# State-space outputs by feature, with decays read back by DMA and two weight triangles as separate products

## What is computed

```python
SSD_HEAD_DIM, SSD_HEADS, SSD_GROUPS, SSD_STATE, SSD_CHUNK = 64, 32, 8, 128, 128

def ssd_chunked(x, dt, a, bm, cm, h0, need_y):
    xc = x * dt[..., None]                              # by chunk of 128 tokens
    cs = jnp.cumsum(dt * a, axis=chunk_tokens)
    ...
    seg = cs[:, :, :, None] - cs[:, :, None, :]
    lmat = jnp.exp(jnp.where(lower, seg, -jnp.inf))
    cb = jnp.einsum('bclgn,bcsgn->bclsg', cc, bc)
    y = (jnp.einsum('bclsg,bclsgr,bcsgrp->bclgrp', cb, lmat, xc)
         + jnp.einsum('bclgn,bcgrpn,bclgr->bclgrp', cc, h_in, jnp.exp(cs)))

def ssd_output(yf, yb, xs, z, ssd_d, ssd_norm_g, w_ssd_o):
    y = (yf + yb + ssd_d[:, None] * xs).reshape(b, n, SSD_D_INNER)
    return rmsnorm(y * jax.nn.silu(z), ssd_norm_g) @ w_ssd_o
```

## Time and profile before

| | |
|---|---|
| median of 3 runs | 2561.36 us (2559.42 to 2563.14) |
| the profiled execution | 2561.69 us, span 2559.9 us |
| TensorE (PE) busy | 2478.0 us, 97% |
| weight loads (PEld) | 2146.7 us, 84% |
| GpSimd (POOL) busy | 1495.2 us, 58% |
| VectorE (DVE) busy | 1224.3 us, 48% |
| ScalarE (ACT) busy | 1125.1 us, 44% |
| DMA | 314.03 MB, 123 GB/s in the mean |
| granted TensorE clock | 0.992 of full |

### The profile page before, as it was taken

How to read it: one execution, slowest core, us unless ns; L and a number is a source line. 1 busy time by engine, 2 the same in 40 slices (tenths; PEclk the granted TensorE clock), 3 DMA queues, 4 the chain that set the end, 5 groups by cost and what they waited for, 6 DMA issues and landing times.

```text
span 2559.9 us, 38883 instructions
## 1 busy us (share of the span) xinstructions
PE 2478.0 (97%) x15118; PEld 2146.7 (84%) x15118; DVE 1224.3 (48%) x2582; ACT 1125.1 (44%) x2371; POOL 1495.2 (58%) x1318
## 2 busy tenths in 40 slices
PE   8999999999899999999999999999989999989998
PEld 7779998885688888888888888888958888889997
DVE  3545502236747888874233112121365788843311
ACT  2345533115526777674022002042364766654543
POOL 1019775870354554543985888865314666668786
PEclk9999999999999999999999999999999999999999
DMA  7566453237532222214322333333463233265554
GB/s 211 181 188 187 133 156 112 83 95 259 194 99 67 75 58 66 75 50 156 95 87 83 99 99 99 99 99 99 133 201 99 83 99 91 69 150 171 168 200 140
DMA packets 365718, 314.03 MB, mean 123 GB/s; under 512 B 13648, under 2 KB 342386, under 8 KB 364530
## 3 DMA queue, kind: packets, MB, share of 16 engines
q1 hardware_dynamic: 361586, 298.80, 39.2%
q10 hardware_dynamic: 3392, 12.59, 1.3%
q0 software_dynamic: 576, 0.43, 0.2%
HBM read 304.45 MB, written 7.34 MB: 122 GB/s over the span
## 4 chain that ended last, share of the span: by engine, by line
PE 81%; DVE 7%; issue 4%; POOL 3%; DMA 2%; ACT 2%; POOLq 0%; SPq 0%; DVEq 0%; ACTq 0%
PE PS L729 39%; PE PS L1131 10%; PE PS L787 5%; PE PS L1138 4%; PE PS L1361 3%; POOL rounded L2767 3%; PE PS L752 3%; DVE mid_a L2489 2%; PE PS L1172 2%; PE PS L1259 2%; PE PS L680 2%; PE PS L1181 2%; PE PS L1059 1%; PE PS L951 1%; PE PS L1047 1%
## 5 line engine op out<-in xcount | busy, mean ns | idle before, releaser
L2767 POOL TENSOR_TENSOR rounded<-ring,rounded 128x512 fp32r<-128x512 f32 (+1 forms) x872 | 1114.3, 1310 | 726.3 <-ACT rounded L1413 415.6
L729 PE MATMUL PS<-rounded 128*128 128x256 f32 (+1 forms) x6096 | 1044.8, 334 | 10.6 <-POOL rounded L2767 7.3
L729 PEld LDWEIGHTS PS<-rounded 128*128 128x128 f32 x6096 | 926.9, 191 | 123.2 <-POOL rounded L2767 6.5
L2790 POOL TENSOR_TENSOR rounded<-ring,constants 128x512 fp32r<-128x512 f32 x216 | 229.3, 1092 | 247.1 <-PE PS L729 124.1
L1131 PE MATMUL PS<-rounded 128*128 128x512 f32 (+1 forms) x1536 | 343.4, 380 | 5.7 <-DVE mid_a L2489 5.1
L1131 PEld LDWEIGHTS PS<-rounded 128*128 128x128 f32 x1536 | 275.4, 188 | 60.8 <-DVE mid_a L2489 3.7
L1413 ACT ACTIVATE rounded<-ring 128x2048 fp32r<-128x2048 f32 (+1 forms) x99 | 180.0, 1822 | 128.9 <-DMA ring<-in_w_mlp_dram 45.7
L2489 DVE SCALAR_TENSOR_TENSOR mid_a<-PS,V,mid_a 128x510 f32<-128x510 f32 (+3 forms) x256 | 182.2, 714 | 25.5 <-ACT mid_a L1742 18.0
L1780 ACT ACTIVATE rounded<-constants,big 128x128 fp32r<-128x128 f32 x384 | 150.2, 391 | 0.0
L1780 ACT ACTIVATE rounded<-constants,mid_v 128x128 fp32r<-128x128 f32 x384 | 150.2, 391 | 0.0
L1138 PE MATMUL PS<-rounded 128*128 128x256 f32 x1152 | 147.7, 286 | 0.0
(11 more groups left out here) (277 smaller groups left out, 3209.8 us busy)
## 6 DMA issues: line engine op xcount, KB each, us to landing
ring<-in_w_mlp_dram SPq DMA_DIRECT2D x64, 1024.0 KB, 5.5
ring<-in_w_in_dram SPq DMA_DIRECT2D x56, 1024.0 KB, 5.4
ring<-in_ada_w_dram SPq DMA_DIRECT2D x48, 1024.0 KB, 5.3
ring<-in_w_in_dram SPq DMA_DIRECT2D x81, 512.0 KB, 4.1
ring<-in_w_up_dram SPq DMA_DIRECT2D x44, 512.0 KB, 5.2
ring<-in_w_ssd_o_dram SPq DMA_DIRECT2D x16, 1024.0 KB, 6.0
ring<-in_w_out_dram SPq DMA_DIRECT2D x12, 1024.0 KB, 5.2
ring<-in_w_down_dram SPq DMA_DIRECT2D x16, 704.0 KB, 4.9
```

What stands on the lines that cost most here:

```text
L729: mm = pe.matmul(PS[:, b, 0:cols], w[:, k, m * P:(m + 1) * P], x(half * kt + k), start=(half == 0 and k == 0 and n_pass == 0), stop=(half ...
L2767: ins = pool.tensor_tensor(lo[:, r], raw[:, r], hi[:, r], ALU.subtract)
L2790: ins = pool.tensor_tensor(hi[:, r], raw[:, r], ones[:, 0:1].broadcast_to([P, 512]), ALU.mult)
```

## The change

The outputs of a chunk are computed with features on partitions. Per head both triangles get a product of their own, and so does each direction's starting state, all added up in one place: the stationary operand is x by token or the starting state, 64 columns wide, the moving one the 128x128 weights. Two heads share a 128-partition result, one in the lower, one in the upper 64 partitions.

The decays come another way. `decay_sums` makes the running sums by head as rows too; they are stored to memory once a layer, and `fetch` reads a group's rows of one chunk back, the same to all 128 partitions. ScalarE makes the exponentials from them: relu(start - row) keeps the argument in bounds (CAP), dt enters as a logarithm. VectorE multiplies by the masked scores, GpSimd multiplies C by the decays of the starting states (`scaled_c`). z is produced by feature; the norm's sums of squares over features are added up by GpSimd (`add_squares`) and summed by one product with ones; its inverse is applied to the gates after the projection rather than before it.

```diff
@@ decays read by DMA
+        decay_sums_of = [nc.dram_tensor(f"decay_sums{l}", (TT, 2 * SSD_HEADS, P), F32, kind="Internal").ap() for l in range(LAYERS)]
+        def decays_of(l, g, t):
+            of_heads = decay_sums_of[l][t].rearrange("(d h) n -> d (h n)", d=2)[:, g * GH * P:(g + 1) * GH * P]
+            return of_heads.unsqueeze(0).broadcast_to([P, 2, GH * P])
@@ TensorE: decay_sums
+                    for d, sums in enumerate((t_le, t_ge)):
+                        r = slice(32 * d, 32 * d + 32)
+                        mm = pe.matmul(PS[r, 4 + t, 256:256 + P], dta[:, t, r], sums, start=True, stop=True)
@@ TensorE: product, z
-                            t0 = (2 * (n - 4) + t) * P
+                            m = (n - 4 + e) * P
-                                    mm = pe.matmul(PS[:, b, t * GW:(t + 1) * GW], x[:, k, t0:t0 + P], w[:, k, :],
+                                    mm = pe.matmul(PS[:, b, e * q_cols:(e + 1) * q_cols], w[:, k, m:m + P], x[:, k, 0:q_cols],
@@ TensorE: seg
-                    for lhs, parts in zip(tri, seg_parts):
-                        for part in parts:
-                            mm = pe.matmul(PS[:, 7 - t % 2, :], lhs, part, start=part is seg_parts[0][0],
-                                           stop=part is seg_parts[1][1])
@@ TensorE: chunk
+                    for j in range(2):
+                        terms = [(xtok[:, t, :], ex[t % 2][:, d, :]) for d in range(2)]
+                        terms += [(hin[:, h, :], decay_rows[rows_of_chunk[t]][:, d, :]) for d, h in starts_of(t)]
+                        for n, (lhs, rhs) in enumerate(terms):
+                            for e in range(2):
+                                r = 2 * j + e
+                                mm = pe.matmul(PS[e * HD:(e + 1) * HD, 7 - j, cols], lhs[:, r * HD:(r + 1) * HD],
+                                               rhs[:, r * P:(r + 1) * P], start=(n == 0), stop=(n == len(terms) - 1))
@@ TensorE: after the last turn
-                pe.wait_ge(*c.need(tok_scaled, ny))
-                for f in range(YT):
-                    turn_scaled(f)
+                pe.matmul(PS[:, 4, 0:q_cols], ones, ctanh_b[:, 0:q_cols], start=True, stop=True).then_inc(*c.made(y_summed))
@@ ScalarE: decays
-                    act.activation(PS[:, 7 - t % 2, :], PS[:, 7 - t % 2, :], ACT.Exp).then_inc(*c.made(e_ready))
-                                act.activation(seg_parts[d][n][:, r * P:(r + 1) * P], mask, ACT.Copy,
-                                               scale=dta_parts[n][:, t, h:h + 1]).then_inc(*c.made(seg_in))
+                    act.wait_ge(*c.sofar(decays_loaded[rows_of_chunk[t]]))
+                    for d in range(2):
+                        for r in range(GH):
+                            h, m = 32 * d + g * GH + r, slice(r * P, (r + 1) * P)
+                            ins = act.activation(ex[t % 2][:, d, m], rows[:, d, m], ACT.Relu, scale=-1.0, bias=start_of[:, t, h:h + 1])
+                    act.activation(ex[t % 2], ex[t % 2], ACT.Exp, scale=-1.0, bias=cap[:, 0:1]).then_inc(*c.made(e_ready))
+                    act.activation(part, part, ACT.Exp).then_inc(*c.made(c_decays))
@@ VectorE: weights and outputs
-                        step(dve.scalar_tensor_tensor(out=m, in0=cb_lo[:, t, :], scalar=dt[:, t, g * GH + r:g * GH + r + 1], in1=m,
-                    dve.tensor_tensor(ex[:, t % 2, :], dt_up[:, t % 2, :], PS[:, 7 - t % 2, :], ALU.mult).then_inc(*c.made(m_ready))
+                    for d, cb in enumerate((cb_lo, cb_up)):
+                        e = per_head(ex[t % 2][:, d, :])
+                        dve.tensor_tensor(e, e, bc_mid(cb[:, t, :], GH), ALU.mult).then_inc(*c.made(g_ready))
+                        dve.scalar_tensor_tensor(out=yg[l][:, f, :], in0=chans[l][p][:, 1 - j, 0:q_cols], scalar=skip_d[:, l, f:f + 1],
+                                                 in1=PS[:, 6 + j, 0:q_cols], op0=ALU.mult, op1=ALU.add).then_inc(*c.made(y_read))
@@ GpSimd: scaled_c
+                            e = per_head(decay_rows[rows_of_chunk[t]][:, d, :])
+                            ins = pool.tensor_tensor(e, e, bc_mid(chans[l][p][:, 3, t * P:(t + 1) * P], GH), ALU.mult)
@@ ScalarE, after the last turn: rounded parts straight from yg, no transposes
+                        act.activation(y_hi[l][:, f, :], yg[l][:, f, :], ACT.Copy, scale=col("ssd_norm_g_2", l * YT + f))\
+                            .then_inc(*c.made(hi_ready))
```

488 lines of the change are left out of this document (241 added, 247 removed).

## The result

| | median, us | runs | ratio to before, 95% interval |
|---|---|---|---|
| before | 2562.1 | 4 | 1 |
| changed | 2534.7 (2533.2 to 2536.8) | 4 | 0.9897 (0.9885 to 0.9910) |

The change makes the kernel 27 us, 1.0%, faster. Forecast were 57.6 us and 2504 us, with a range of 2490 to 2530: the direction was right, half of the gain did not come, and the time lies outside the range. The profiled execution of the changed kernel took 2533.2 us with a span of 2531.4, 28.5 less than before; its stretches are compared here.

What follows compares the result with a forecast made beforehand. TensorE, 81% of the chain, was taken as the bound. Layer 0 turns 27.5, layer 1 turns 9, waits 8, tails 12 and 6.5, less added 3.4 and 2, gave 57.6 us off 2561.7: 2504 us, range 2490 to 2530.

Steps and rivals of the forecast that it cites:

- every cover grows: In the group loops other engines get more slack; VectorE's late convolutions in layer 1 come on time, 8 us gained.
- the turn of layer 0: Sign for layer 0's group loop: a turn of 45.0 us without idle; forecast wrong if not between 44 and 46.
- Side by side: Chunk products: two 64-column halves overlap fully, 0.055 us a record; chunks of 2.06 or 1.62 us, 92 us in all.
- rivals A and B: Chunk halves do not overlap, 2581 us, chance 0.09; or overlap only partly, 2524 us, chance 0.12.
- Rival B: Chunk halves overlap only partly, a step of 0.14 us, streaming 97 us instead of 77; 2524 us, chance 0.12.
- z by feature: Layer 0's z in 48 products of 512 columns: 1.1 us a group, 9 us gained; layer 1 nothing.
- Layer 1's turns: Layer 1's group loop: 1.1 us a group, 9 us, plus 8 us from vanishing waits; turn near 34 us.
- Tail of layer 0: Before layer 0's output projection, token norms and 128 turned products go; 3 us waiting for gate 7's eviction; 12 us gained.
- Tail of layer 1: Before layer 1's output projection, 64 turned products and a wait go; 0 if slabs decide, 6.5 us gain taken.
- Added work: Two 32-column products a chunk for stored sums, 0.42 us each time, 3.4 us; operations before each layer's fence, 2 us.
- rival C: Reading one memory row by 128 partitions is slow, ScalarE waits for decay rows in layer 0; 2544 us, chance 0.07.
- Rival D: Both tails give nothing because ScalarE's and VectorE's copies and rests stand in the open; 2523 us, chance 0.07.

Runs made afterwards that it cites:

- e1: Changed kernel with GpSimd's scaled_c(2) moved ahead of the rests of the next group's slabs in a turn; 2512.6 us, ratio 0.9816.
- e5: Kernel of e4 with all of a chunk's products for the first 64-column half before those for the second, not alternating; 2518.1 us, ratio 0.9828.
- e4: Changed kernel with the moves of e1, e2 and e3 together; 2503.0 us, ratio 0.9766.
- e7: Changed kernel with GpSimd's products of C with decay rows cut to 8 of 128 columns, only time read; 2508.9 us in one run.
- e2: Changed kernel with gate tile 7's eviction in layer 0's tail moved ahead of ScalarE's wait for rests and rounding; 2529.6 us, ratio 0.9867.
- e3: Changed kernel, layer 1's tail: transfers back issued behind the last gained rows, slab 2 rounded after eight rests; 2527.3 us, ratio 0.9866.

## Why the prediction was wrong

**The step that failed** is "GpSimd swaps products of the same size and adds two sums of squares a group. So every cover grows". It looked at what each engine has to do in a turn and not at the order in which GpSimd does it, nor at the new number of products. With an order in which two slab rests stand ahead of a product that TensorE needs first, the cover was gone in six of eight turns: 14.3 us of waiting, of the 17 us that layer 0's loop missed by. e1 gave it back (14.8). The text had named the turn of layer 0 as the test, 44 to 46 us; it was 48.3, and is 45.35 once the order is mended.

**Side by side (rivals A and B).** Refuted as costs of the chunk: 1.90 and 1.46 us are below the 2.06 and 1.62 summed. For two halves in this kernel the records show no loss: a pair of records starts about every 0.11 us (eight records, 992.71 to 993.14), and one record alone takes no less in e5 (four, 994.24 to 994.73). But the forecast's evidence was misread. The 3.6 times for L680 set a row's length (12 records of 256 columns in 2.75 us) against starts; by starts those 12 take 2.40 us, 1042.26 to 1044.66, so 0.20 each and 3.2 us for 16, which against L680's 1.01 is 3.2 times for four. Rival B drew on the Trainium skill, page "TensorE: Matmul & The Clock Gate", section "Measured speedup vs the span model", with 2.38 times for three column tiles, which is 79% of ideal. The trace agrees with that share for four, 3.2 of 4 being 80%, where the prediction said that it did not.

**z by feature** was mis-sized. 3.22 + 3.22 us were the lengths of rows, tails included, though the text itself warns of them. By starts the term is 0.7 us a turn and not 1.1. All pieces of a turn by starts, before and in e4: the sums give 4.2 us, the chunks cost 1.1 (5.6 before, 6.7 after), z gives 0.6, and the four other input products cost 0.6 more (22.1 before, 22.7 after), three of them next to split products. That makes 3.1 (48.4 to 45.35) where 3.4 were summed; over the loop 25.1 (e1) of 27.5. So what the chunks are cheaper than forecast is paid by their neighbours.

**Layer 1's turns** gave 13.6 of 17 us. The turn is near the forecast 34 (34.3), but the waits for VectorE did not go (3.4 us of 5.1 left), because VectorE does not get the relief that was summed: its weights were bounded by 0.62 and 1.08 us and take 1.36 in layer 0 and 1.18 in layer 1, above the upper bound, with GpSimd busy beside it; and the last step of silu, which the change does not touch, went from 1.10 to 1.39 us on `ctanh_b` and from 1.12 to 1.31 on `constants` in layer 1. e7 shows the coupling. In the last turn new waits of 2.4 and 2.0 us stand where those of 1.7 and 1.0 were.

**Tail of layer 0.** Forecast 12, measured 10.8. The mechanism was the one named, gate 7's eviction behind the rests; the wait was 5.5 and not 3, and 4.15 us of it were program order (e2).

**Tail of layer 1.** Forecast 6.5, measured 1.5. The lower bound, 0 "if slabs decide", was the right case. The step missed that the transfers back stand behind VectorE's last rest and meet the slabs there; with them issued early the tail gives 7.4 (e3, 50.2 to 42.8). Which of the three makes the slabs late was not tested; the windows above speak for the 4 KB of the last gate.

**Added work.** The 32-column sums cost 0.46 us each where 0.42 were summed (from the sums to the next projection product 1.50 us after, L1107 to L739, against 1.04 before, L1097 to L729). The fence cost nothing in place of 2: from the last sums to the loop it takes 3.7 us with 0.34 of new products in it, against 3.5 before, and in layer 1 it is shorter.

**The fetch (rival C)** cost nothing, as forecast: ScalarE has no wait for it, and the median landing time is 4.9 us for 512 KB, against 4.1 in the earlier trace rows. **Rival D**, tails without gain, came true in one tail of two.

**The clock** was in no term. TensorE was granted half clock for 42.7 us of the profiled execution before and for 61.7 after, 19.0 more, which is at most 9.5 us of lost work. Of these 19.0 us 5.1 lie in the 8 tiles, 10.2 between them and layer 1's loop, and 4.7 in the end; the tails have 2.4 more and the first row 3.4 less. In the last two the clock fits the growth of 3.5 and 2.7 us: e4, with 10.2 and 5.2 us at half clock there against 13.7 and 5.1 before, takes 627.1 and 242.6 us, as before. In the 8 tiles it does not, for they stay at 134.3 us with the clock full (e2, e4); there the late rests cost as much. The mean granted clock was 0.992 in the profiled execution before; of the four runs after none was above 0.988, and in e4, without the new waits, all five stood at 0.991. In e1, without those of layer 0's loop, it went from 0.986 to 0.990, so the waits are not the whole of it.

With the three orders mended (e4) the kernel takes 2503.0 us; the forecast of 2504 was for a kernel without them. That it lies so close is partly luck: the sum had 3 to 4 us too much for z and the same for layer 1's waits and nothing for the late rests in the 8 tiles (2.4), and too little for the tails (14.9 us in layer 0 and 8.5 in layer 1 in e4) and the fence.

## What to carry to other kernels

Where work moves to an engine that had slack, follow that engine's program order through one turn and ask when each result is due; a sum of its busy time does not show a product that stands behind work for the next turn. Ask the same of transfers: when they can be issued, and what else wants the DMA engines then. A wait that names the engine that prepares a weight slab may only pass on a late landing, so test it by moving the transfer and the preparation apart. And where several transfers are moved together, time them apart as well: the small one may be the one that costs.
